# A gate tile kept ahead of the linear attention's states, and a last product computed in two halves of the tokens

## What is computed

```python
h = h + 0.5 * swiglu(rmsnorm(h, ffn1_norm), ffn1_w_gate, ffn1_w_up, ffn1_w_down)
h = h + token_mixing(rmsnorm(h, mix_norm), w_in, ...)      # [linear attention | sparse attention] @ w_out
h = h + 0.5 * swiglu(rmsnorm(h, ffn2_norm), ffn2_w_gate, ffn2_w_up, ffn2_w_down)
return rmsnorm(h, final_norm)[:, 16:]                      # drop the meta tokens
```

```python
S_new = exp(b_last) * S + sum_j (k_j * exp(b_last - b_j)) v_j
o = rmsnorm(q * exp(b) @ S + intra_chunk, head_norm) * silu(r)
```

## Time and profile before

| | us |
|---|---|
| median of 3 runs | 1074.19 (1073.76 to 1074.44) |
| profiled execution | 1071.18 |
| its span | 1069.4 |
| TensorE matmuls busy | 1043.1 (98% of the span) |
| TensorE weight loads busy | 943.3 (88%) |
| VectorE busy | 778.1 (73%) |
| GpSimd busy | 657.3 (61%) |
| ScalarE busy | 466.5 (44%) |
| mean granted TensorE clock | 0.994 of 2.4 GHz |

### The profile page before, as it was taken

How to read it: one execution, slowest core, us unless ns; L and a number is a source line. 1 busy time by engine, 2 the same in 40 slices (tenths; PEclk the granted TensorE clock), 3 DMA queues, 4 the chain that set the end, 5 groups by cost and what they waited for, 6 DMA issues and landing times. The chain is left out here.

```text
span 1069.4 us, 19548 instructions
## 1 busy us (share of the span) xinstructions
PE 1043.1 (98%) x7439; PEld 943.3 (88%) x7439; DVE 778.1 (73%) x1247; ACT 466.5 (44%) x739; POOL 657.3 (61%) x744
## 2 busy tenths in 40 slices
PE   7999999999999999999999999999899999999997
PEld 6999999999999998788767677778799999999986
DVE  5737897687676588599675586478889977777835
ACT  7434444344343354552255526453434433443425
POOL 3948677787776367079721203356777877777840
PEclk8999999999999999999999999999999999999999
DMA  6333334424432444344321101223233434334322
GB/s 189 91 93 87 88 109 117 112 71 114 113 89 81 118 106 117 87 101 118 99 61 40 41 21 60 70 69 89 70 99 99 119 109 114 88 105 109 89 59 79
DMA packets 172256, 98.69 MB, mean 92 GB/s; under 512 B 6787, under 2 KB 167606, under 8 KB 172166
## 3 DMA queue, kind: packets, MB, share of 16 engines
q1 hardware_dynamic: 172064, 97.38, 32.3%
q10 hardware_dynamic: 102, 0.08, 0.0%
HBM read 91.18 MB, written 2.10 MB: 87 GB/s over the span
## 5 line engine op out<-in xcount | busy, mean ns | idle before, releaser
L1775 POOL TENSOR_TENSOR wl<-raw,wh 128x256 fp32r<-128x256 f32 x292 | 250.1, 892 | 224.3 <-ACT wh L1880 186.0
L1775 POOL TENSOR_TENSOR wxl<-raw,wxh 128x256 fp32r<-128x256 f32 x240 | 230.1, 984 | 150.2 <-ACT wxh L1880 149.7
L2360 PE MATMUL ps<-ah,wxh 128*128 128x264 f32 (+1 forms) x456 | 122.0, 322 | 2.8 <-DVE h L2171 2.4
L2360 PE MATMUL ps<-ah,wxl 128*128 128x264 f32 (+1 forms) x456 | 121.7, 321 | 0.0
L2360 PE MATMUL ps<-al,wxh 128*128 128x264 f32 (+1 forms) x456 | 121.5, 321 | 0.0
L2171 DVE SCALAR_TENSOR_TENSOR h<-ps,h 128x528 f32<-128x528 f32 (+1 forms) x96 | 66.5, 693 | 70.0 <-PE ps L2360 70.0
L2360 PE MATMUL ps<-xh,wh 128*128 128x264 f32 (+3 forms) x336 | 102.5, 348 | 2.3 <-DVE h L2171 1.1
L2479 PE MATMUL ps<-xh,wh 128*128 128x264 f32 (+1 forms) x360 | 101.9, 283 | 0.9 <-DVE h L2171 0.9
L2479 PE MATMUL ps<-xl,wh 128*128 128x264 f32 (+1 forms) x360 | 101.9, 283 | 0.0
L2479 PE MATMUL ps<-xh,wl 128*128 128x264 f32 (+1 forms) x360 | 101.5, 282 | 0.0
L2360 PE MATMUL ps<-xl,wh 128*128 128x264 f32 (+3 forms) x336 | 97.3, 332 | 0.0
(11 more groups left out here) (316 smaller groups left out, 2968.8 us busy)
## 6 DMA issues: line engine op xcount, KB each, us to landing
raw<-in_ffn_w_gate SPq DMA_DIRECT2D x44, 512.0 KB, 4.1
raw<-in_ffn_w_up SPq DMA_DIRECT2D x44, 512.0 KB, 4.3
raw<-in_ffn_w_down SPq DMA_DIRECT2D x80, 256.0 KB, 2.8
raw<-in_w_in SPq DMA_DIRECT2D x28, 512.0 KB, 4.1
raw<-in_w_out SPq DMA_DIRECT2D x8, 512.0 KB, 3.4
xin<-in_x SPq DMA_DIRECT2D x4, 512.0 KB, 5.8
raw<-in_ffn_w_down SPq DMA_DIRECT2D x16, 128.0 KB, 2.2
out<-xin SPq DMA_DIRECT2D x4, 512.0 KB, 3.6
```

What stands on the lines that cost most here:

```text
L1775: op = pool.tensor_tensor(dst[:, part], src[:, part], high[:, part].bitcast(F32), ALU.subtract)
L2360: mm = pe.matmul(ps[0:m, bank + a, 0:width], places(lo, PLACE[u], -(-WIDTH[u] // HALF_UNIT))[:, k * P:k * P + m], r[:, tile, t:t + width], ...
```

## The change

Three edits. In VectorE's round `g == 3` the last gate tile (`keep_fill(7)`) is taken out before `states()` instead of behind it. The last tile (`d` = 7) of the second feed-forward's last down product is made in two halves of 256 tokens, in banks 4 and 5, with an addition, a square and a scaling of 256 columns for each; its square is no longer added to `ss` by VectorE, and TensorE sums it straight from `t01`, with a second matmul behind that of `ss` for each token block. And ScalarE takes a square root of a scrap value before tile 3's square, which loads the root's table there; the later root finds it loaded.

```diff
--- before.py
+++ after.py
@@ -467,6 +467,9 @@
             c, w = x_cols(2 * t)
             return [(a, max(c, a * HALF) - a * HALF, slice(max(c, a * HALF) - c, min(c + w, (a + 1) * HALF) - c))
                     for a in range(2) if max(c, a * HALF) < min(c + w, (a + 1) * HALF)]
+        LAST_HALVES = [(0, META), (1, META + SEQ // 2)]
 
         def keep_y(eng, half):
 
@@ -1553,8 +1556,9 @@
                     out_lo(last)
                     keep_fill(6)
                 if g == 3:
+                    keep_fill(7)
                     states()
-                    keep_fill(7)
 
             def add_early(d):
                 dve.wait_ge(w_used, Q_USED[U_OUT + (d - 4) // 2])
@@ -2003,10 +2007,21 @@
                 for d in range(KT):
                     if d == 1:
                         hi(U_DOWN[number, last, KT - 1])
+                    if number and d == 3:
+                        act.activation(scrap[:, :], scrap[:, :], ACT.Sqrt).then_inc(scrap_done, 1)
                     if number == 0:
                         if d >= 6:
                             hi(U_MIX + d - 6)
                         prep_hi(1, d, hd + d)
+                    if number and d == KT - 1:
+                        for a, t in LAST_HALVES:
+                            part = slice(t, t + SEQ // 2)
+                            act.wait_ge(h_done, hd + d + a + 1)
+                            act.wait_ge(ss_done, 4 * KT - 2)
+                            act.activation(t01[:, d % 2, part], h[:, d, part], ACT.Square).then_inc(sq_done, 1)
+                            act.activation(h[:, d, part], h[:, d, part], ACT.Copy, scale=gains[:, 3, d:d + 1]).then_inc(y_done, 1)
+                        continue
                     square(norm + 1, d, hd + d)
                     if number:
 
@@ -2285,9 +2300,15 @@
                     add_down(*step_down_of(g, m, 1))
 
                 for d in range(KT + 1):
-                    if d < KT:
+                    if number and d == KT - 1:
+                        for a, t in LAST_HALVES:
+                            dve.wait_ge(w_used, Q_USED[U_DOWN[number, last, d]] + a)
+                            part = h[:, d, t:t + SEQ // 2]
+                            dve.scalar_tensor_tensor(out=part, in0=ps[:, down_bank(last, d) + a, 0:SEQ // 2], scalar=0.5,
+                                                     in1=part, op0=ALU.mult, op1=ALU.add).then_inc(h_done, 1)
+                    elif d < KT:
                         add_down(last, d)
-                    if d:
+                    if d and not (number and d == KT):
                         if number == 0:
                             prep_lo(norm + 1, d - 1)
                         prep(norm + 1, d - 1)
@@ -2492,6 +2513,14 @@
                                 pe.wait_ge(c_add, 6 * (n + 1))
                             else:
                                 pe.wait_ge(h_done, hd + KT * last + (d - 3 if d else 0))
+                        if number and d == KT - 1:
+                            for a, t in LAST_HALVES:
+                                for k in range(cnt):
+                                    mm = product_k(v, down_bank(last, d), P, ah, al, order[last][k] % 4, order[last][-1] % 4 + 1, order[last][k], norm,
+                                                   [(a, t, SEQ // 2)], order[last][0] % 4)
+                                mm.then_inc(w_used, 1)
+                            continue
                         down(v, down_bank(last, d), order[last], norm, k0, k1, ft + GROUPS[last][0] if d == 0 else None)
 
             pe.wait_ge(consts, 2)
@@ -2539,14 +2568,17 @@
                 half, t = divmod(n, 4)
                 tokens = slice(META + t * P, META + (t + 1) * P)
                 if n == 4:
-                    pe.wait_ge(ss_done, 4 * KT)
+                    pe.wait_ge(ss_done, 4 * KT - 1)
+                    pe.wait_ge(sq_done, 4 * KT + 1)
                     for c in range(4):
-                        mm = pe.matmul(ps[:, 7, c:c + 1], ss[:, META + c * P:META + (c + 1) * P], ones[:, 0:1],
-                                       start=True, stop=True)
+                        part = slice(META + c * P, META + (c + 1) * P)
+                        pe.matmul(ps[:, 7, c:c + 1], ss[:, part], ones[:, 0:1], start=True, stop=False)
+                        mm = pe.matmul(ps[:, 7, c:c + 1], t01[:, (KT - 1) % 2, part], ones[:, 0:1], start=False, stop=True)
                     mm.then_inc(norm_sum, 1)
                 if n == 7:
                     pe.wait_ge(var_done, 4)
-                pe.wait_ge(y_done, 4 * (half + 1))
+                pe.wait_ge(y_done, (4, KT + 1)[half])
                 for k in range(4):
                     mm = pe.transpose(ps[:, n, k * P:(k + 1) * P], h[:, 4 * half + k, tokens], ident[:, :])
                 mm.then_inc(y_turned, 1)
```

## The result

| | before | after |
|---|---|---|
| median, us | 1073.93 (8 runs, 1071.35 to 1074.44) | 1077.32 (8 runs, 1076.49 to 1077.92) |
| profiled execution / its span, us | 1071.18 / 1069.4 | 1077.92 / 1076.2 |
| mean granted TensorE clock | 0.994 | 0.989 |

The changed kernel is slower by 3.4 us: the ratio is 1.0036, with a 95% interval of 1.0027 to 1.0044. That is beyond 0.2% and outside the predicted range.

What follows compares the result with a forecast made beforehand. TensorE's matmuls were taken as busy for 98% of the span, with VectorE the bound before level 5. Middle 0, wait and start -0.5 (product's +0.08 included), added matmuls +0.91: +0.4 on 1074.19, giving 1074.6 us, range 1072.6 to 1075.5.

Steps and rivals of the forecast that it cites:

- The middle, at full clock: Gate tile ahead of the states: TensorE wins 1.91 us, then waits 2.3 us before level 5; net 0.
- The clock: Rival, 5%: TensorE's 2.3 us idle before level 5 lowers its clock, 5.1 us lost, 1079.7 us.
- The median lies 3.0 us above that execution and I move it by the same: Step from the profiled execution, 1071.18 us, to the median: 1074.19 before, 1074.6 forecast after.
- The product in halves: Last product as 24 matmuls of 256 columns, 0.119 us apart: first transpose 0.08 us later.
- Wait and squares: Before the final sum: the 0.48 us wait goes, sum starts some 0.5 us earlier (bounds 0.3 and 0.55).
- The added matmuls: In TensorE's final sum: eight more records at 0.114 us each, +0.91 us on the path (0.8 to 1.05).
- Sum of the end: Last product to final sum: wait and start -0.5 us, including the product's +0.08, added matmuls +0.91; +0.4 us.
- The root's table: Table load moved ahead of tile 3's square: that square about 0.9 us late but covered, price 0.
- The middle's gain comes through: Rival, 10%: level 5 could start with TensorE, not VectorE, so 1.91 us are won, 1072.7 us.
- The squares are late: Rival at the end: sum starts no earlier, tail costs +0.91 + 0.1, 1075.2 us; within the forecast's 77% as upper end.

Runs made afterwards that it cites:

- the split idle time: The whole change, but TensorE waits for the states at L873 too, against the kernel before: 1073.88 us (12 runs), ratio 1.0008.
- the additions ahead: Kernel before, with VectorE adding down products 2 and 3 to `h` ahead of two low parts in the second feed-forward: 1071.45 us, ratio 0.9985.

## Why the prediction was wrong

*The middle, at full clock*: right. It said that TensorE wins 1.91 us and waits 2.3 us ahead of level 5, ended by L1478, and that level 5 doesn't move. Measured: 2.30 and 2.34 us, ended by that line, and a shift of 0.00 and 0.01 us. VectorE's unbroken column was the right thing to read.

*The clock*: this is the step that failed. The sum took the middle at 0, which needs the clock to stay at 1.00 behind the 2.3 us of idle time, and gave its fall 5%. It fell, and the middle cost 3.15 us. The two traces that have the idle stretch show it, and the mean clocks (none of 19 executions at 0.994) fit it in every execution. It is also the sign of being wrong that the prediction named, a clock under 1.00 between 640 and 1060. The rival's price, 5.1 us, was too high because it charged 10.3 us at half clock, as at the start; here the clock was low for 6.8 us. About half of the low time is lost in either sum. The argument against the rival was that the clock had stayed at 1.00 at 769 to 770, inside a wait of 2.36 us. That was one execution; behind just this wait the clock fell in five of nine traces. A fall that one trace doesn't show is no evidence that the same idle time is safe.

The Trainium skill's "TensorE: Matmul & The Clock Gate", section "Part 1: The HAM clock gate (the \"warmup\" mystery)", says that throttled is the default state and activity lifts it. The traces agree as far as that goes: behind 2.30 us of idle time the granted clock was 0.84 from 648 to 650 and 0.50 from 650 to 652, and with TensorE at work it came back.

*"The median lies 3.0 us above that execution and I move it by the same"*: this step had the warning in it and passed over it. Three microseconds between the profiled execution and three runs that agree within 0.7 was the sign of something that comes and goes.

*The product in halves*: right. 24 matmuls 0.12 us apart, the transposes 2.85 us behind the first instead of 2.78 (+0.07 for +0.08).

*Wait and squares*: right in kind; additions and squares of 256 columns lasted 0.42 each, near the low end, and the sum starts 0.65 - 0.07 = 0.58 us earlier for 0.5, just past the upper bound of 0.55.

*The added matmuls*: near the forecast. The sum takes 0.80 us more than before, for 0.91, and 0.88 more than the eight records without a wait ahead of them; the sixteen records stand 1.71 / 16 = 0.107 us apart. Sum of the end: +0.21 for +0.4. The Trainium skill ("TensorE: Matmul & The Clock Gate", section "Back-to-back issue gap") gives about 25 ns for a matmul of so few columns; for these records, each with a weight load of its own, the measured 0.107 us decides.

*The root's table*: right. It was loaded at 1053.37, the square of tile 3 started at 1054.77, and nothing behind it was late: the addition of tile 4 waited 1.48 us for TensorE's product, as before, and its square for that addition:

```profile
1053.37 1.28 ACT L2012 ACT_TABLE_LOAD   x1
```

*The middle's gain comes through*, the rival with 10%, did not happen: level 5 didn't move. *The squares are late* did not happen either: no wait stands ahead of the sum.

## What to carry to other kernels

Removing a wait from the busiest engine gains nothing if a later wait on the same slower engine takes it up, and two short waits put together into one can cost the clock: before moving work, add up the idle time that TensorE will have at one place, and put real work there. Compare the profiled execution's time and mean clock with those of the other executions; where they differ by more than those spread, compare executions of like clock. And a sum moved to another engine has to be priced against the wait that it removes: here 0.8 us of matmuls for a start 0.6 us earlier, where VectorE's sum of the halves gave the same start without them.

## What the runs showed of the hardware

The granted clock was lowered to 0.50 behind idle stretches of TensorE of about 2 us, with work at full clock before them. Behind 2.30 and 2.34 us ahead of level 5 it fell in both traces that have this wait; behind 1.9 us, at 639 to 644, in three traces (the change without its first edit, the split idle time, the additions ahead) and not in the four others that have it; behind 2.36 us near 772, in five traces of nine. In one trace the fall came 0.2 us before TensorE worked again, in the others 0.3 to 1.4 us after. The clock then stayed low for 3.4 us at 639 and at 772 and for 6.8 us at level 5, with TensorE busy, and 3.15 of the 6.8 us were lost. Why one execution falls and the next doesn't was not tried.
